# Two SwiGLU down projections as a seven-product 2x2 block product, with two smaller reorderings

## The chip, the core and the metric

The kernel runs on 1 core of one Trainium2 chip. The metric is the device time in microseconds (us) of one launch. TensorE (PE) multiplies, VectorE (DVE), ScalarE (ACT) and GpSimd (POOL) work elementwise, SyncE (SP) issues most of the DMAs. Each engine runs its own queue strictly in order; between engines only semaphores count.

## What is computed

Two transformer-like blocks over 1024 tokens of width 1024, float32. The part that the change rewrites stands at the end of each block:

```python
D_FF = ((8 * D_MODEL + 3 * 256 - 1) // (3 * 256)) * 256          # 2816
def _swiglu(h, w_gate, w_up, w_down):
    return (jax.nn.silu(h @ w_gate) * (h @ w_up)) @ w_down
# block 1
x_new = x_new + g2 * _swiglu(_modulate(x_new, norm_ffn_w[layer], sh2, sc2), w_ffn_gate[layer], w_ffn_up[layer], w_ffn_down[layer])
# block 2: the same form, with h = rms_norm(x) * (1 + sc2) + sh2
x = x + g2 * ((jax.nn.silu(h @ ffn_w_gate[l]) * (h @ ffn_w_up[l])) @ ffn_w_down[l])
```

Two smaller parts are touched too: `hyena_filters` (a small network of sines whose filters are windowed, squared and summed over 1024 positions) and the first norm of block 2, `rms_norm(x) * (1 + sc1) + sh1`.

## The kernel before

Activations lie feature-major: 8 tiles (KT) of 128 features by 1024 tokens, and tokens are cut into two halves of 512 (HALF). The hidden width is 22 tiles (FT). Every float32 product is made of three matmuls of rounded parts: high weights by high activations, high by low, low by high. ACT makes a high part with a rounding copy, DVE makes the low part by subtracting it from the raw tile, so a raw tile always passes ACT and then DVE before PE may use it.

**Gate and up projections** (class `Quad`, used by both ffn stages). For n from 2 to 21 the gate and up product of hidden tile n is already a 2x2 block product with seven products, each of 12 matmuls, in the order p1, p6, p2, p7, p5, p4, p3 on three PSUM banks per n. POOL forms the weight sums of n + 1 (`sums_s124`) and of n + 2 (`sum_s3`) and adds some products to others (lines 2311, 2313, 2315). ACT copies products out of the banks (`copy`, line 2395), because PE adds the next product into the same bank: p4 waits for the copy of p7, p3 for the copy of p5. ACT also applies the silu of token half 0 right after p2 (line 2416); it stands ahead of the copies of p7 and p5. The two hidden halves of n come out on DVE (`direct_out`, `second`), and SP stores each to DRAM (`ffn_hidden`, line 2293). In SP's loop over n the loads of weights for n + 2 stand ahead of the stores of n.

**Down projection** (function `ffn`). It runs in NS = 22 steps: 11 pairs of hidden tiles for token half 0, then 11 for half 1. A step loads 1024 KB of weights (line 2533) and 512 KB of hidden rows (line 2535) into one of three slots; ACT rounds them (`parts_high`, lines 2588 and 2589), DVE makes the low parts (`split`, lines 2611 and 2613), and PE does 48 matmuls of 128x512 (8 output tiles m, 2 hidden tiles, 3 parts) into 8 banks, line 2574 to 2576. The load of step n waits for the end of step n - 3. Steps 0 to 2 are loaded and in part split while `Quad` still runs its last n. After 11 steps DVE adds the 8 banks to x (`evict`, line 2633) and ACT and DVE begin the squares of the next norm. x itself was put aside in DRAM, and one DMA of 4096 KB brings it back right after the load of step 7 (line 2540).

In ffn_1 (block 1) POOL also issues `cond_row` (a row of 512 KB) and 24 DMAs of 1024 KB (`condition_space`, line 2550): the modulation vector of block 2 is computed in the shadow of the down projection, ACT making one silu (line 2593) and DVE two reductions per group (`modulate`, line 2624). ACT's silu stands in its queue between the parts of step 1 and those of step 2. POOL then stores the finished x to `x_kept`, 16 DMAs.

**Start of block 2** (`block_2`, stage "projections"): ACT rounds three loaded weight groups (`proj.highs`) and then the normed x (`norm_2.take_high`); DVE makes the low weight parts (`proj.lows`, line 2971), then scales half 0 of x (line 622), makes its low part (line 626), and does the same with half 1.

**Filter network** (`filter_network`, woven into stage "modulation_1"): for each of 8 position chunks c PE fills banks 4 and 5 (line 826), DVE windows them (line 874), ACT squares them (line 848), PE sums the squares (line 833). The matmul of chunk c waits until DVE has read the banks of chunk c - 1; DVE's write of chunk c waits until the DRAM stores of chunk c - 2 have landed, since the difference is formed in place.

## Time and profile before

| | us |
|---|---|
| median of 3 runs | 3599.43 (3591.16 to 3603.64) |
| the profiled execution | 3592.82, span of its instructions 3590.8 |
| PE busy | 3312.8 (92% of the span), mean granted clock 0.945 |
| DVE, ACT, POOL busy | 1763.1, 1190.3, 553.0 |
| DMA | 366.16 MB, 102 GB/s over the span |

The page gives for every engine its busy time, for every line and tile a group of instructions, and who ended the idle time ahead of it. A matmul's duration there (389 ns) is longer than the distance from one matmul to the next, because matmuls are pipelined, so a stage is costed by the distance.

### The profile page before, as it was taken

How to read it: one execution, taken by the hardware profiler on the slowest of the kernel's cores; microseconds unless marked ns; L12 is line 12 of the kernel's file. 1: busy time of each engine (PE TensorE's matmuls, PEld its weight loads, DVE VectorE, ACT ScalarE, POOL GpSimd, SP SyncE). 2: the span in 40 equal slices, each digit the busy share in tenths (PEclk: the TensorE clock that was granted, in tenths of full speed). 3: DMA queues.
4: the chain of work that ended last, by engine and by line, in shares of the span. 5: the costliest groups of instructions: out<-in, count | busy, mean ns of one | idle time of the engine just before them, and what ended most of it. 6: DMA issues, size and time to landing. Idle time of an engine off the chain costs nothing. (4 is left out here: it accounts for less than half of the span.)

```text
span 3590.8 us, 38285 instructions
## 1 busy us (share of the span) xinstructions
PE 3312.8 (92%) x15192; PEld 2476.6 (69%) x15192; DVE 1763.1 (49%) x2758; ACT 1190.3 (33%) x1829; POOL 553.0 (15%) x560
## 2 busy tenths in 40 slices
PE   7999998988899999999998998888878899999997
PEld 4476544444778778888886777565456678888886
DVE  6447535446323374433576634444665474443344
ACT  3326522212422253333233332441220253333232
POOL 3100000000100024554001010011000025544000
PEclk8999997996899999999999999998989899999999
DMA  5430010000332232223775123233324132222533
GB/s 225 170 129 13 10 36 13 13 13 1 128 120 93 94 109 82 81 87 110 266 271 216 44 70 93 80 108 118 76 94 158 54 103 81 87 81 96 199 141 117
DMA packets 109945, 366.16 MB, mean 102 GB/s; under 512 B 13991, under 2 KB 33447, under 8 KB 91720
## 3 DMA queue, kind: packets, MB, share of 16 engines
q1 hardware_dynamic: 72056, 244.24, 19.3%
q0 software_dynamic: 21056, 111.05, 8.2%
q10 hardware_dynamic: 16656, 8.42, 1.3%
q8 instruction: 121, 1.98, 0.2%
q14 instruction: 56, 0.46, 0.0%
HBM read 300.63 MB, written 63.05 MB: 101 GB/s over the span
## 5 line engine op out<-in xcount | busy, mean ns | idle before, releaser
L2574 PE MATMUL banks<-hidden_high,down_high 128*128 128x512 f32 x704 | 274.9, 390 | 3.8 <-DVE x L2633 3.8
L2576 PE MATMUL banks<-hidden_high,down_low 128*128 128x512 f32 x704 | 273.9, 389 | 0.0
L2575 PE MATMUL banks<-hidden_low,down_high 128*128 128x512 f32 x704 | 273.9, 389 | 0.0
L1585 PE MATMUL banks<-work,weight_ring 128*128 128x512 f32 (+1 forms) x640 | 264.9, 575 | 0.5 <-ACTq L4296 0.5
L2144 POOL TENSOR_TENSOR quad_raw<-quad_raw 128x512 f32<-128x512 f32 x160 | 229.6, 1436 | 126.4 <-DMA quad_raw<-in_w_gu 120.2
L2276 PE MATMUL banks<-block_t_high,quad_low 128*128 128x512 f32 x608 | 236.5, 389 | 0.0
L2611 DVE TENSOR_TENSOR down_low<-down_raw,down_high 128x2048 fp32r<-128x2048 f32 x44 | 100.9, 2292 | 237.0 <-ACT down_high L2588 237.0
L1585 PEld LDWEIGHTS banks<-work,weight_ring 128*128 128x128 f32 x640 | 126.6, 200 | 130.1 <-issue 124.7
L2588 ACT ACTIVATE down_high<-down_raw 128x2048 fp32r<-128x2048 f32 x44 | 84.4, 1918 | 317.2 <-DMA hidden_raw<-ffn_hidden 317.2
L1767 DVE SCALAR_TENSOR_TENSOR x<-x,work,banks 128x128 f32<-128x128 f32 x320 | 111.3, 348 | 142.9 <-PE banks L1611 132.4
L2274 PE MATMUL banks<-block_t_high,quad_high_b 128*128 128x512 f32 x456 | 177.6, 390 | 0.4 <-ACT quad_partial L2395 0.3
L2275 PE MATMUL banks<-block_t_low,quad_high_b 128*128 128x512 f32 x456 | 177.4, 389 | 0.0
L2276 PE MATMUL banks<-block_b_high,quad_low 128*128 128x512 f32 x456 | 177.4, 389 | 0.0
L2395 ACT ACTIVATE quad_partial<-banks 128x512 f32<-128x512 f32 x160 | 95.6, 598 | 241.9 <-PE banks L2276 236.1
L2574 PEld LDWEIGHTS banks<-hidden_high,down_high 128*128 128x128 f32 x704 | 132.2, 188 | 32.3 <-DVE hidden_low L2613 4.6
L2575 PEld LDWEIGHTS banks<-hidden_low,down_high 128*128 128x128 f32 x704 | 132.2, 188 | 27.8 <-issue 0.5
L2576 PEld LDWEIGHTS banks<-hidden_high,down_low 128*128 128x128 f32 x704 | 132.1, 188 | 27.5
L2944 PE MATMUL banks<-mix_high,ring_parts 128*128 128x512 f32 x320 | 134.8, 421 | 13.6 <-DVE ring_parts L2971 4.6
L2474 DVE TENSOR_TENSOR quad_gated<-banks,quad_partial 128x512 f32<-128x512 f32 x40 | 27.7, 692 | 229.6 <-PE banks L2276 224.6
L2194 DVE TENSOR_TENSOR quad_low<-quad_raw,quad_high_a 128x1536 fp32r<-128x1536 f32 x44 | 79.4, 1804 | 106.3 <-POOL quad_raw L2144 104.9
L2276 PEld LDWEIGHTS banks<-block_t_high,quad_low 128*128 128x128 f32 x608 | 114.2, 188 | 23.8
L2945 PE MATMUL banks<-mix_low,ring_parts 128*128 128x512 f32 x320 | 129.2, 404 | 0.0
(607 smaller groups left out, 7497.6 us busy)
## 6 DMA issues: line engine op xcount, KB each, us to landing
down_raw<-in_w_down SPq DMA_DIRECT2D x44, 1024.0 KB, 4.9
quad_raw<-in_w_gu SPq DMA_DIRECT2D x40, 768.0 KB, 4.3
condition_space<-in_mod_w POOLq DMA_DIRECT2D x24, 1024.0 KB, 6.2
ffn_hidden<-quad_gated SPq DMA_DIRECT2D x88, 256.0 KB, 2.0
hidden_raw<-ffn_hidden SPq DMA_DIRECT2D x44, 512.0 KB, 5.9
weight_ring<-in_w_merge SPq DMA_DIRECT2D x24, 512.0 KB, 3.7
quad_raw<-in_w_gu SPq DMA_DIRECT2D x48, 256.0 KB, 3.1
weight_ring<-in_dft SPq DMA_DIRECT2D x12, 1024.0 KB, 5.4
```

The lines of the kernel that those rows point to most:

```text
L1585: mm = e.matmul(pg.ps[:, bank_of(h, n), 0:b - a], slot[:, (2 * k + t) * P:(2 * k + t + 1) * P], h1[:, k, a:b], start=(k == 0), stop=(k == ...
L1767: ins = e.scalar_tensor_tensor(out=S[:, 8 * d + (q + 1) % 8, :], in0=S[:, 8 * d + q % 8, :], scalar=dec[:, d, 4 * t + c:4 * t + c + 1], in ...
L2144: e.tensor_tensor(self.weight(n, out), self.weight(n, a), self.weight(n, b), op).then_inc(self.sums.sem, 1)
L2274: e.matmul(bank, w_hi[:, k], hi[:, k], start=(start and k == 0), stop=False, skip_group_check=again)
L2275: e.matmul(bank, w_hi[:, k], lo[:, k], start=False, stop=False, skip_group_check=again)
L2276: mm = e.matmul(bank, w_lo[:, k], hi[:, k], start=False, stop=(k == 3), skip_group_check=again)
L2574: e.matmul(bank, wh[:, k, m], hh[:, k], start=(p == 0 and k == 0), stop=False)
L2575: e.matmul(bank, wh[:, k, m], hl[:, k], start=False, stop=False)
L2576: mm = e.matmul(bank, wl[:, k, m], hh[:, k], start=False, stop=(p == NP - 1 and k == 1))
L2611: e.tensor_tensor(wl, raw, wh.bitcast(F32), ALU.subtract).then_inc(low.sem, 1)
L2944: e.matmul(bank, w_hi[:, c], MH[:, k, t], start=start, stop=False)
L2945: e.matmul(bank, w_hi[:, c], ML[:, k, t], start=False, stop=False)
```

## The change

**The down projection.** The 1024 outputs are cut into two halves of 512 (4 tiles), each pair of hidden tiles into its two members, the tokens into their two halves. The product of a 2x2 block of weights with a 2x2 block of hidden values is formed with seven block products instead of eight, in four phases of 11 steps (NS = 44): phases 0, 1 and 2 do two products per step (24 matmuls), phase 3 one (12 matmuls). Slots go from three to four; the load of step n waits for the end of step n - 4.

- While `Quad` runs, POOL forms four block combinations of the hidden values for each pair of n (`turn_hidden`), SP stores seven blocks of 256 KB per pair instead of four. The even n's hidden tiles get buffers of their own (`even`), and before these are written again, `out_free` waits for the four combinations and for the stores of the pair.
- POOL forms the weight combinations: two subtractions per step in phase 0, one in phases 2 and 3, none in phase 1 (`weight_sums`). One of phase 0 is stored by SP to DRAM (`down_sum`) and loaded again in phase 3. The load of step n, for n from 4 to 14, waits until the `down_sum` of step n - 4 has been stored; that store is issued right behind the load of step n - 1.
- A step loads 1280 KB in phase 0 (and stores 256 KB), 1024 KB in phases 1 and 2, 768 KB in phase 3.
- After phases 0, 1 and 2 ACT copies the 8 banks out (`stage_products`, 24 copies), POOL adds them to each other (`fold`, 12 additions in its queue at step 23), and DVE adds the results to x (`onto`) at steps 24 to 27, 35, 36 and 38; four banks are added directly at the end.
- x comes back behind the load of step 14. The 24 condition groups are spread one per step over steps 4 to 10, 12 to 21 and 26 to 32; `cond_row` is issued behind the last `turn_hidden`. POOL's `x_kept` stores stand at steps 30 and 41 and at the end.

**The filter network** uses two pairs of banks in turn and a tile of its own for the difference (`filter_bank`, `DIFF`): the matmul of chunk c waits for DVE's read of chunk c - 2, and the wait for the stores stands only ahead of the sum. The modulation's four groups then share two banks, and are read out inside DVE's loop.

**The norm of block 2**: ACT takes the high parts of half 0 ahead of the weights' high parts, and DVE scales half 0 ahead of `proj.lows`, and half 1 behind the low part of half 0.

```diff
@@ Quad
+        self.turned_hidden.wait(e, 4 * (n // 2))            # out_free
+        if s == 0:
+            self.stored[0].wait(e, 16 * (n - 1))
+        else:
+            self.stored[1].wait(e, 80 * (n // 2))
@@ Quad.sync
-            for s in range(2):
-                self.out[s].wait(e, n + 1)
-                e.dma_start(self.hidden[n, :, s * HALF:(s + 1) * HALF], self.pg.gated[:, 2 + s, :]).then_inc(self.stored[s].sem, 16)
+            to = self.hidden[n // 2]
+            self.out[0].wait(e, n + 1)
+            e.dma_start(to[:, BLOCK_21 if n % 2 else BLOCK_11, :], self.out_tile(n, 0)).then_inc(self.stored[0].sem, 16)
+            if n % 2:
+                self.out[1].wait(e, n + 1)
+                e.dma_start(to[:, BLOCK_22, :], self.out_tile(n, 1)).then_inc(self.stored[1].sem, 16)
+                t1, t2, t4 = self.pg.turned
+                for i, (block, tile) in enumerate(((BLOCK_T1, t1), (BLOCK_T2, t2), (BLOCK_T3, self.pg.even[:, 1, :]), (BLOCK_T4, t4))):
+                    self.turned_hidden.wait(e, 4 * (n // 2) + i + 1)
+                    e.dma_start(to[:, block, :], tile).then_inc(self.stored[1].sem, 16)
@@ Quad.pool
+            if n % 2 == 0:
+                self.turn_hidden(e, n - 1)
             self.copied.wait(e, 4 * i + 2)
             e.tensor_tensor(s6, s1, s6, ALU.add).then_inc(self.joined.sem, 1)
...
+            if n == FT - 1:
+                down_sums(e, 1)
+                down_sums(e, 2)
+        self.turn_hidden(e, FT - 1)
@@ Quad.scalar
             self.products.wait(e, self.done(n, "p2"))
-            self.stored[0].wait(e, 16 * n)
-            e.activation(pg.gated[:, 2, :], self.bank(n, 0), ACT.Silu).then_inc(self.silu_1.sem, 1)
+            self.out_free(e, n, 0)
+            e.activation(self.out_tile(n, 0), self.bank(n, 0), ACT.Silu).then_inc(self.silu_1.sem, 1)
             copy(n, 2, "p7")
             copy(n, 3, "p5")
@@ ffn, sync
+                step_done(e, n - SLOTS)
+                if n - SLOTS < NP:
+                    s2_stored.wait(e, 16 * (n - SLOTS + 1))
...
         for n in range(3, NS):
             load(e, n)
-            if n == 7:
+            if n - 3 < NP:
+                sums.wait(e, 2 * (n - 3) + 2)
+                e.dma_start(s2[n - 3], pg.down[(n - 3) % SLOTS][0][:, 2, :]).then_inc(s2_stored.sem, 16)
+            if n == 14:
                 e.dma_start(x, x_kept).then_inc(x_back.sem, 16)
@@ ffn, tensor
+            for i, (wh, w_low, bh, b_low) in enumerate(products):
+                for m in range(4):
...
+                    elif p == 0 and phase:
+                        staged.wait(e, 8 * (phase - 1) + at + 1)
+                    c = slice(m * P, (m + 1) * P)
+                    e.matmul(bank, wh[:, c], bh, start=(p == 0), stop=False)
+                    e.matmul(bank, wh[:, c], b_low, start=False, stop=False)
+                    mm = e.matmul(bank, w_low[:, c], bh, start=False, stop=(p == NP - 1))
@@ block_2, vector
+        norm_2.scale_half(e, 0)
         proj.lows(e, 0)
         norm_2.take_low(e, 0)
+        norm_2.scale_half(e, 1)
         norm_2.take_low(e, 1)
```

Three places where instructions stand in another order now, each of ffn_1 where `Quad` hands over to the down steps. Names such as `projection_full` or `to_fm_sums` in brackets are semaphores that several stages share.

SP's queue there. Before: `ffn_hidden` rows are the hidden stores, `down_raw` and `hidden_raw` the loads.

```order
131 L2533 DMA down_raw_91<-in_w_down 128x2048 [waits projection_full]
132 L2535 DMA hidden_raw_92<-ffn_hidden 128x2x512 [waits chunk_rows_spread_0]
133 L2533 DMA down_raw_97<-in_w_down 128x2048 [waits projection_full]
134 L2535 DMA hidden_raw_98<-ffn_hidden 128x2x512 [waits chunk_rows_spread_0]
135 L2533 DMA down_raw_103<-in_w_down 128x2048 [waits projection_full]
136 L2535 DMA hidden_raw_104<-ffn_hidden 128x2x512 [waits chunk_rows_spread_0]
137 L2293 DMA ffn_hidden<-quad_gated 128x512 [waits chunk_outputs]
138 L2293 DMA ffn_hidden<-quad_gated 128x512 [waits chunk_products]
139 L2533 DMA down_raw_91<-in_w_down 128x2048 [waits projection_group_used]
140 L2535 DMA hidden_raw_92<-ffn_hidden 128x2x512 [waits chunk_rows_spread_0]
141 L2533 DMA down_raw_97<-in_w_down 128x2048 [waits projection_group_used]
```

After: the `ffn_blocks` stores come from the hidden tiles and from the combinations (`hidden_turned`, waiting for `to_fm_sums`), `columns_raw` is the hidden block's load, and `down_sum` the stored weight combination.

```order
169 L2323 DMA ffn_blocks<-quad_gated 128x512 [waits chunk_outputs]
170 L2326 DMA ffn_blocks<-quad_gated 128x512 [waits chunk_products]
171 L2330 DMA ffn_blocks<-hidden_turned_116 128x512 [waits to_fm_sums]
172 L2330 DMA ffn_blocks<-hidden_turned_117 128x512 [waits to_fm_sums]
173 L2330 DMA ffn_blocks<-even_hidden 128x512 [waits to_fm_sums]
174 L2330 DMA ffn_blocks<-hidden_turned_118 128x512 [waits to_fm_sums]
175 L2605 DMA down_raw_106<-in_w_down 128x1024 [waits projection_full]
176 L2606 DMA down_raw_106<-in_w_down 128x512
177 L2620 DMA columns_raw_107<-ffn_blocks 128x1024 [waits chunk_rows_spread_1]
178 L2626 DMA down_sum<-down_raw_91 128x512 [waits to_fm_ready]
179 L2605 DMA down_raw_91<-in_w_down 128x1024 [waits chunk_rows_spread_0,projection_group_used]
180 L2606 DMA down_raw_91<-in_w_down 128x512
```

The load of step 3 (`down_raw_106`) now stands behind six stores of which four wait for POOL, and from there on a store stands behind every load, and the next load waits for it (`chunk_rows_spread_0`).

POOL's queue at the same place. Before: the last additions of `Quad`, then the condition DMAs.

```order
202 L2311 TENSOR_TENSOR quad_partial<-quad_partial 128x512 [waits projection_read]
203 L2313 TENSOR_TENSOR quad_partial<-quad_partial 128x512 [waits projection_read]
204 L2315 TENSOR_TENSOR quad_partial<-quad_partial 128x512 [waits chunk_summed]
205 L2546 DMA condition_space<-in_cond_rows 128x1024 [waits projection_full]
206 L2550 DMA condition_space<-in_mod_w 128x2048 x2
207 L2550 DMA condition_space<-in_mod_w 128x2048 [waits modulation_used] x22
```

After: `down_raw` rows are the weight combinations of steps 1, 2, 3 and 4.

```order
247 L2638 TENSOR_TENSOR down_raw_96<-down_raw_96 128x512 [waits projection_loaded_1]
248 L2640 TENSOR_TENSOR down_raw_96<-down_raw_96 128x512 [waits to_fm_ready]
249 L2638 TENSOR_TENSOR down_raw_101<-down_raw_101 128x512 [waits projection_loaded_2]
250 L2640 TENSOR_TENSOR down_raw_101<-down_raw_101 128x512 [waits to_fm_ready]
251 L2372 TENSOR_TENSOR hidden_turned_116<-even_hidden 128x512 [waits chunk_rows_spread_1,chunk_products,chunk_outputs]
252 L2374 TENSOR_TENSOR hidden_turned_117<-quad_gated,hidden_turned_116 128x512 [waits to_fm_sums]
253 L2375 TENSOR_TENSOR even_hidden<-quad_gated,even_hidden 128x512
254 L2377 TENSOR_TENSOR hidden_turned_118<-quad_gated,hidden_turned_117 128x512 [waits to_fm_sums]
255 L2672 DMA condition_row<-in_cond_rows 128x1024 [waits chunk_products,projection_full]
256 L2667 DMA condition_space<-in_mod_w 128x2048
257 L2638 TENSOR_TENSOR down_raw_106<-down_raw_106 128x512 [waits projection_loaded_3]
258 L2640 TENSOR_TENSOR down_raw_106<-down_raw_106 128x512 [waits to_fm_ready]
```

The condition row is issued behind the combinations of steps 1 and 2 and behind `turn_hidden`.

ACT's queue at the same place. Before:

```order
609 L2588 ACTIVATE down_high_100<-down_raw_97 128x2048 [waits projection_loaded_1]
610 L2589 ACTIVATE hidden_high_102<-hidden_raw_98 128x1024
611 L2399 ACTIVATE quad_gated<-quad_gated 128x512 [waits chunk_states]
612 L2593 ACTIVATE condition_space<-condition_space 128x1024 [waits condition_loaded]
613 L2588 ACTIVATE down_high_106<-down_raw_103 128x2048 [waits projection_loaded_2]
614 L2589 ACTIVATE hidden_high_108<-hidden_raw_104 128x1024
```

After:

```order
609 L2730 ACTIVATE down_high_100<-down_raw_96 128x1024 [waits to_fm_ready,projection_loaded_1]
610 L2731 ACTIVATE down_high_100<-columns_raw_97 128x1024
611 L2457 ACTIVATE quad_gated<-quad_gated 128x512 [waits chunk_states]
612 L2750 ACTIVATE condition_row<-condition_row 128x1024 [waits condition_loaded]
613 L2730 ACTIVATE down_high_105<-down_raw_101 128x1024 [waits to_fm_ready,projection_loaded_2]
614 L2731 ACTIVATE down_high_105<-columns_raw_102 128x1024
```

The order is the same; what moved is what the fourth row waits for: the DMA of the condition row, now behind POOL's `turn_hidden`, stands ahead of the parts of step 2 (`down_high_105`).

## Rows read from the trace of the kernel before

**Rows 1.** Windows of down stages: us, busy (count) by engine, clock, DMA share, GB/s.

```profile
1706.60:1948.40 241.80, 240.32 (x1058) 198.34 (x1057) 150.91 (x189) 69.88 (x59) 20.90 (x39) 1.00 0.70 264
1862.00:1894.00 32.00, 32.00 (x143) 26.51 (x142) 26.73 (x38) 8.60 (x6) 3.19 (x6) 1.00 0.92 351
3383.30:3402.40 19.10, 19.10 (x86) 15.83 (x85) 3.43 (x2) 2.87 (x2) 0.00 (x0) 1.00 0.96 384
1964.10:1968.10 4.00, 3.98 (x10) 3.16 (x11) 4.00 (x7) 4.00 (x7) 0.00 (x0) 0.51 0.03 6
```

**Rows 2.** Groups: busy, mean ns, idle before. Middle row: one line, min/median/max ns.

```profile
L2574 PE MATMUL banks<-hidden_high,down_high 128*128 128x512 f32 x704 | 274.9, 390 | 3.8 <-DVE x L2633 3.8
...
L2144 POOL TENSOR_TENSOR quad_raw<-quad_raw x160: 1279/1293/3415, 1305.7 to 3293.1; 128x512 f32<-128x512 f32 x160
...
L2624 DVE CUSTOM_DVE_ANT_0 condition_space<-condition_space 128x1024 f32<-128x1024 f32 x48 | 58.7, 1223 | 1.5 <-DMA condition_space<-in_mod_w 0.6
```

**Rows 3.** Timelines (start us, us, engine, line), one down step of ffn_2.

```profile
3483.14 0.33 SPq L2533 DMA_DIRECT2D down_raw<-in_w_down  x1
...
3494.02 0.33 SPq L2533 DMA_DIRECT2D down_raw<-in_w_down  x1
...
3489.45 1.92 ACT L2588 ACTIVATE down_high<-down_raw 128x2048 fp32r<-128x2048 f32 x1 [8.15 <-DMA hidden_raw<-ffn_hidden]
3491.28 1.04 ACT L2589 ACTIVATE hidden_high<-hidden_raw 128x1024 fp32r<-128x1024 f32 x1
...
3493.61 1.22 DVE L2613 TENSOR_TENSOR hidden_low<-hidden_raw,hidden_high 128x1024 fp32r<-128x1024 f32 x1
```

**Rows 4.** DMA issues: operation, engine, count, KB each, median us to landing.

```profile
ffn_hidden<-quad_gated SPq DMA_DIRECT2D x88, 256.0 KB, 2.0
...
x<-ffn_x SPq DMA_DIRECT2D x1, 4096.0 KB, 19.2
```

**Rows 5.** Timelines of one n in ffn_1: POOL, DVE, ACT.

```profile
1668.70 4.35 POOL L2144 TENSOR_TENSOR quad_raw<-quad_raw 128x512 f32<-128x512 f32 x3 [1.20 <-DMA quad_raw<-in_w_gu]
...
1673.15 1.76 DVE L2194 TENSOR_TENSOR quad_low<-quad_raw,quad_high_a 128x1536 fp32r<-128x1536 f32 x1 [2.61 <-POOL quad_raw L2144]
1676.23 2.29 DVE L2194 TENSOR_TENSOR quad_low<-quad_raw,quad_high_b 128x2048 fp32r<-128x2048 f32 x1 [1.32 <-ACT quad_high_b L2183]
...
1676.51 0.60 ACT L2416 ACTIVATE quad_gated<-banks 128x512 f32<-128x512 f32 x1 [0.32 <-PE banks L2276]
1679.23 0.60 ACT L2395 ACTIVATE quad_partial<-banks 128x512 f32<-128x512 f32 x1 [2.12 <-PE banks L2276]
```

**Rows 6.** Timelines, POOL and DVE at once, start of ffn_1.

```profile
1305.71 10.13 POOL L2144 TENSOR_TENSOR quad_raw<-quad_raw 128x512 f32<-128x512 f32 x4 [25.08 <-DMA quad_raw<-in_w_gu]
...
1307.89 3.39 DVE L2445 TENSOR_TENSOR block_b<-block_b,block_t 128x2048 f32<-128x2048 f32 x1
```

**Rows 7.** Timelines, start of ffn_1's down stage (DVE, ACT, POOL, SP).

```profile
1710.60 0.69 DVE L2464 TENSOR_TENSOR quad_gated<-quad_gated,quad_partial 128x512 f32<-128x512 f32 x1 [0.70 <-ACT quad_gated L2399]
...
1711.75 1.06 ACT L2593 ACTIVATE condition_space<-condition_space 128x1024 f32<-128x1024 f32 x1 [1.18 <-DMA condition_space<-in_cond_rows]
...
1707.32 0.58 POOL L2546 DMA_DIRECT2D condition_space<-in_cond_rows  x1 [2.02 <-PE banks L2276]
...
1717.93 0.33 SPq L2533 DMA_DIRECT2D down_raw<-in_w_down  x1
```

**Rows 8.** Timelines, start of block 2's projections (DVE, PE).

```profile
1957.71 2.58 DVE L2971 TENSOR_TENSOR ring_parts<-weight_ring,ring_parts 128x1024 fp32r<-128x1024 f32 x2 [4.46 <-ACT ring_parts L2963]
...
1962.47 5.38 DVE L622 SCALAR_TENSOR_TENSOR x<-x,parameters,work 128x512 f32<-128x512 f32 x8
...
1964.12 0.76 PE L2926 MATMUL banks<-mix_high,ring_parts 128*128 128x512 f32 x1 [10.01 <-ACT mix_high L612]
```

**Rows 9.** Timeline of PE in the filter network's loop.

```profile
30.40 3.78 PE L826 MATMUL banks<-work 64*128 64x512 f32 x4 [7.18 <-ACT work L842]
35.63 3.78 PE L826 MATMUL banks<-work 64*128 64x512 f32 x4 [1.45 <-DVE work L874]
```

414 lines of the change are left out of this document (283 added, 131 removed).

## The prediction, made before the changed kernel had run

> **What bounds the kernel now.** I read the windows of the down stages first. In ffn_1's down stage PE is busy 240.3 of 241.8 us, so the stage is bound by its matmuls; DMA is busy 0.70 at 264 GB/s on average [rows 1]. But in a stretch of the same stage in which x and condition groups arrive, DMA is busy 0.92 at 351 GB/s, and where x comes back in ffn_2 it is 0.96 at 384 GB/s: 7.34 MB in 19.1 us, the most that this trace shows. The groups then say what one operation costs: a matmul group of 704 waits 3.8 us in all, for DVE's eviction; a POOL sum of 128x512 takes 1.29 us, 3.4 at the longest; a modulation reduction on DVE 1.22 us [rows 2]. The timeline of one down step gives the pace: loads are issued 10.88 us apart, 48 matmuls, so 0.2267 us each. It also gives the round trip: issued at 3483.14, ACT begins at 3489.45, 6.3 us for 1.57 MB; ACT takes 1.04 and DVE 1.22 us per 1024 columns [rows 3]. A store of 256 KB lands after 2.0 us, x after 19.2 [rows 4]. So the products are worth their full time only if loads, POOL, ACT and DVE keep pace with a shorter stage.
>
> **1. Products.** 22 steps of 48 are 1056 matmuls per stage; 33 steps of 24 and 11 of 12 are 924. 2 x 132 x 0.2267 = **-59.8 us**. PE's down stages would fall from 239.4 to 209.5 each.
>
> **2. The loop over n, even n from 2 to 20.** In one n whose PE step begins at 1668.15, POOL's three sums end at +4.9, DVE's two low parts (1.76 and 2.29) begin there and at +8.1, ACT's silu is at +8.4 and the copy of p7 at +11.1 [rows 5]. New behind POOL's sums are the four operations of `turn_hidden`, 5.2 us, and ACT's silu of an even n waits for all four. POOL and DVE operations with two inputs in SBUF take turns: four POOL sums took 10.13 us while DVE was back to back, where 4 x 1.29 = 5.2 was due, and a DVE operation of 2048 columns took 3.39 against 2.29 [rows 6]. Taking turns, the four and the two low parts end at 4.9 + 5.2 + 4.05 = +14.1; silu and copy of p7 follow, to +15.3. PE wants bank 2 for p4 after five products of 12: 60 x 0.2267 = +13.6. Stall 1.7 per even n, 20 in both ffns: 34. If POOL is not held up its four end at +10.1 and nothing is late: 0. Rows 6 is the nearest row, but there DVE left no gap; I take three quarters, **+25** (0 to +34).
> The Trainium skill (SBUF — State Buffer, Who interferes with whom) says that a DVE instruction with two SBUF inputs and a GpSimd instruction that reads SBUF exclude each other for the whole instruction, and that issue order decides who blocks. Rows 6 agree in the sum and leave the order open. By the rule the term is 34 if DVE comes between, and 0 if POOL's four go first.
>
> **3. Start of the down stage (T0 = 1707.05, one step ahead of the load of step 3).** The last hidden half is out at T0 + 4.3 [rows 7]. After the change the second half of 21 waits for more on DVE and POOL, I take T0 + 6.5; four turned blocks with DVE between, as in 2, end near T0 + 14. The load of step 3 stands behind them on SP: issued at 14.3. Then landing 5.5 (6.3 scaled to less data, upper part latency), POOL's two subtractions 2.6, ACT 2.1, DVE 2.4, of which some overlap: ready at 26.4. PE wants step 3 after 3 x 5.44 = 16.3. ffn_2: **+10** (5 to 12). In ffn_1 the condition row, issued at 1707.32 with its silu at 1711.75 [rows 7], is now issued at T0 + 14; its silu stands on ACT ahead of the parts of step 2, behind which are all later parts. 14 + 4.4 + 1.1 + 2.1 + 2.3 = 23.9 for step 2, due at 10.9: **+13** (8 to 16). Load 3 is ready in its shadow.
>
> **4. Phase 0.** A load waits for the store behind the load before it, so data do not queue: load and store, 1.57 MB, make one round trip of 6.3 us per step [rows 3] where PE wants 24 x 0.2267 = 5.44. 7 steps x 0.86 = **+6** for ffn_2 (0 to 12). In ffn_1 a 1 MB group comes with each step: 2.62 MB at 384 GB/s are 6.8 us, and DVE (2 x 1.22 for the group, 2.4 to split) shares its port with POOL's 2.6. I take 8 us per step: 7 x 2.5 = **+17** (10 to 25).
>
> **5. x comes back** behind load 14. 4.2 MB at 384 GB/s are 10.9 us. The loads behind have no lead left after 4; in ffn_2 a step of phase 1 needs 2.7 us of transfer and has 5.44, so half of it is regained: **+5** (0 to 11). In ffn_1 load and group are 2.1 MB, 5.46 us, so nothing is regained, and the rest of the row competes: **+14** (5 to 16).
> The Trainium skill (DMA: Bandwidth & Descriptors, Specifications) gives about 358 GB/s for one core's share of HBM. Rows 1 show 384, so the measurement decides; by the page's figure each 2.1 MB would take 5.9 us, and this term with the one before about 8 us more.
>
> **6. Sums on POOL.** At its step 23 stand 12 additions, 15.6 us, ahead of the weight sum of step 24. The copies start them about 1 us into step 22; sum, ACT and DVE follow (4.6): ready at +21, due at +10.9. What of the copies' lead and of DVE's reads can be regained I put at 3: **+7** each, +14 (6 to 20). Phase 2 of ffn_1 has, at steps 26 to 28, split 2.4, reductions 2.45, additions of x 2 x 0.6 and more on DVE, and 1.3 on POOL, over 5.44: **+8** (0 to 12). Phase 3 has steps of 2.72 us in which DVE has 1.8 and POOL 1.3, and four additions or squares, and eight spills of POOL, stand between: **+9** for both (3 to 15).
> The stage boundaries: three times one ACT copy (0.60) per ffn, 3.6, for the 3.8 us that the eviction cost [rows 2]: 0.
>
> **7. Norm and filter.** DVE's three low parts of weights stand ahead of the scaling of half 0, which begins at 1962.47 and can begin near 1953, when ACT's and DVE's first group is done; PE waits 10.0 us there [rows 8]. The high parts of the weights now come later, so that of the wait only about 4 go: **-3.9** (-8 to 0). PE restarts at a clock of 0.51 of the full 2.4 GHz (the 1.2 GHz level) for 4 us after that idle time [rows 1]. In the filter loop PE's 3.78 us are followed by 1.45 of waiting for DVE [rows 9]; with two pairs of banks it goes, but ACT and DVE then set the pace: **-1.5** (-6 to 0).
>
> **Sum:** -59.8 + 25 + 10 + 13 + 6 + 17 + 5 + 14 + 14 + 8 + 9 - 3.9 - 1.5 = +55.8. The profiled execution is 3592.8 (span 3590.8 and 2 around it), 6.6 under the median of 3599.4, inside the runs' spread. 3592.8 + 55.8 = 3648.6; against the median, which I forecast, **3655**.
>
> **Rivals.**
> *B. Half of the waits.* POOL's four go first (2 becomes 0), and the four slots cover a part of 4 and 5: waits 75 of 121, with -65 that is +10: 3605 to 3615. For it: a POOL sum is 1.29 us in the median, with 3.4 as rare end [rows 2], so POOL is seldom held up. Against: its sums are ahead of DVE's parts there, `turn_hidden` stands beside them.
> *C. Faster: the saving stands.* Its place is the load of step 3 and the chain of loads and stores behind it. It decides if load 3 is issued by T0 + 8, and a load and its store together land within 5.44 us: a store of 256 KB alone lands after 2.0 [rows 4], and it waits in SP's queue only for a POOL sum done long ago. Then 4 is 0, 3 is 8 in all, 5 is 8, 2 is 0, and 6 half, 16: 32 against -65.2, **3566**. If ffn_1 is then bound by its bytes (47.9 MB of blocks, 25 of groups, 8 of x, 81 at 384 GB/s: 211 us for 209.5) that adds 2. Against it: the 6.3 us of rows 3 hold for 1.57 MB whoever asks.
> *D. The transfers bind ffn_1 over its whole length.* 81 MB at the 351 GB/s of the mixed stretch are 231 us, 21 over PE's 209.5, on top of a late start: with 2 and 6 in full, 3690 or more.
> *E. The change does not do what it says:* 132 matmuls fewer per ffn are countable, so only in that a clock fall after the new waits takes from the rest: over 10 us of waiting costs 4 us at 0.51 again, in 3, twice: +4.
>
> **How the numbers follow.** My case, most waits in full, 3620 to 3700: 0.55. B 0.15, of which half lies within 0.3% (10.8 us, about what a measurement of this kernel can tell from no change). C 0.22, D 0.06, E's addition 0.02. Faster by over 0.3%: C and a little of B, **0.24**; within: **0.08**; slower: **0.68**. Both signs have weight, so: the likeliest case alone is 3620 to 3700; the range leaves the lower half of C and the end of D out: **3563 to 3694**.
>
> **What will show it.** PE's count in the down lines must fall by 264. Term 2: idle of PE ahead of p4 on ACT's copy of p7 in even n, and `turn_hidden` operations well over 1.3 us. Term 3: a gap on PE at T0 + 16.3 in ffn_2 of about 10, and in ffn_1 at T0 + 10.9 of 13, ended by DVE's low parts. Term 4: loads issued 6.3 and 8 us apart in phase 0, each right after a store has landed; if they are 5.44 apart the term is 0. Term 5: a gap near steps 15 to 18, DMA at 0.95. Term 6: a gap at step 24 behind POOL. Term 7: PE's wait at block 2 down from 10 to 6. The prediction is wrong if PE's idle time inside the down stages is under 40 us, or in the loop over n under 5.

## The result: 3730 us, 3.8% slower

The changed kernel takes 3730.4 us (median of 4 runs, 3723.7 to 3734.7) against 3595.3 for the kernel before: 1.0375 times its time, 95% interval 1.0341 to 1.0409. Slower was the likelier forecast, but the time lies above the range; the change costs 135 us where the sum said 56. The experiments below find where the 135 us went; no kernel with the seven-product down projection, however mended, came under the kernel before.

The page of after, first its engine line and two groups of part 5 (busy, mean ns | idle ahead, releaser), then a DMA row (KB, us to landing):

```profile
PE 3307.7 (89%) x14928; PEld 2453.4 (66%) x14928; DVE 1871.4 (50%) x2900; ACT 1238.3 (33%) x1965; POOL 884.0 (24%) x760
...
L2710 PE MATMUL banks<-down_high 128*128 128x512 f32 x616 | 259.9, 422 | 123.9 <-DVE columns_low L2781 87.8
...
L2304 PE MATMUL banks<-block_t_high,quad_high_b 128*128 128x512 f32 x456 | 179.8, 394 | 17.2 <-ACT quad_partial L2453 17.2
...
condition_space<-in_mod_w POOLq DMA_DIRECT2D x24, 1024.0 KB, 8.2
```

PE has 264 matmuls fewer, as meant, and is hardly less busy (3307.7 us for 3312.8). Ahead of the down matmuls it idles 123.9 us, where the group of before had 3.8 [rows 2], and one matmul takes 422 ns in the mean for 390, since a part of them ran at the low clock (the stages' mean granted clock is 0.89 and 0.93, where before it was 1.00). The windows of the two down stages (columns as in [rows 1]):

```profile
1723.20:2036.00 312.80, 238.40 (x927) 187.35 (x925) 198.82 (x259) 99.53 (x128) 98.99 (x96) 0.89 0.72 255
3436.00:3712.80 276.80, 227.24 (x927) 180.92 (x926) 133.70 (x139) 99.95 (x129) 80.41 (x57) 0.93 0.55 184
```

ffn_2's before, which [rows 1] do not show:

```profile
3327.90:3570.50 242.60, 240.24 (x1059) 198.28 (x1058) 89.39 (x69) 68.70 (x57) 0.00 (x0) 1.00 0.39 143
```

ffn_1's down stage took 241.8 us before [rows 1] and takes 312.8, and ffn_2's went from 242.6 to 276.8. From the starts of the stages in the two traces, the 142.1 us between the spans (3590.8 and 3732.9) are: everything up to the first gate and up product, the filter network in it, -2.4; gate and up projections +18.7 and +18.8; ffn_1's down stage with the norm behind it +68.8; the untouched rest of block 2 +4.1; ffn_2's down stage with the tail +34.1.

**Excess.** A step of the down stage has an ideal length (24 matmuls of 0.2267 us, 5.44 us; in phase 3 it is 12, 2.72 us). What the distance between two steps' first matmuls is over that is called its excess here, low clock included. It is worked out from the start of every step in the trace, and summed over steps:

```
steps          0-3   4-10  11-13 14-22 23-25 26-32 33-43  all
after   ffn_1 17.1   34.6   2.0  17.5  13.0   6.2  12.9  103.4
        ffn_2 15.2   20.1   1.9   5.1  13.3   0.0  11.5   67.2
```

That is 170.6 us of excess for 59.8 us of matmuls saved (an execution of `silu_behind`, whose down stages are the same code, has 168.8). A delay is counted in the step ahead of the matmul that it holds: an excess in step 10 is a late start of step 11. In between, steps run at exactly 5.44: the product saving is real, and it is lost at named places.

### The profile page after: what moved, and what is told of

Read it like the earlier page. It is cut to its first block and busy times, and to the rows that moved or that the text cites. A ratio compares the mean times of both kernels' runs of the same rounds, so it can differ in the third digit from the quotient of the medians.

```text
span 3732.9 us, 38599 instructions
## 1 busy us (share of the span) xinstructions
PE 3307.7 (89%) x14928; PEld 2453.4 (66%) x14928; DVE 1871.4 (50%) x2900; ACT 1238.3 (33%) x1965; POOL 884.0 (24%) x760
## 5 line engine op out<-in xcount | busy, mean ns | idle before, releaser
L2710 PE MATMUL banks<-down_high 128*128 128x512 f32 x616 | 259.9, 422 | 123.9 <-DVE columns_low L2781 87.8
L2711 PE MATMUL banks<-columns_low,down_high 128*128 128x512 f32 x616 | 252.6, 410 | 0.0
L2712 PE MATMUL banks<-down_high,down_low 128*128 128x512 f32 x616 | 252.2, 409 | 0.0
L2710 PEld LDWEIGHTS banks<-down_high 128*128 128x128 f32 x616 | 123.8, 201 | 166.2 <-DVE columns_low L2781 97.2
L2304 PE MATMUL banks<-block_t_high,quad_high_b 128*128 128x512 f32 x456 | 179.8, 394 | 17.2 <-ACT quad_partial L2453 17.2
L1781 DVE SCALAR_TENSOR_TENSOR x<-x,work,banks 128x128 f32<-128x128 f32 x320 | 111.3, 348 | 139.2 <-PE banks L1625 128.7
L2730 ACT ACTIVATE down_high<-down_raw 128x1024 fp32r<-128x1024 f32 x66 | 69.8, 1057 | 322.6 <-POOL down_raw L2640 135.1
L2224 DVE TENSOR_TENSOR quad_low<-quad_raw,quad_high_a 128x1536 fp32r<-128x1536 f32 x44 | 97.4, 2213 | 106.2 <-POOL quad_raw L2174 104.9
L1868 POOL DMA_DIRECT2D branches<-work x32 | 17.3, 541 | 557.1 <-ACT work L1939 554.7
L3145 PE MATMUL banks<-mix_high,ring_parts 128*128 128x512 f32 x320 | 137.1, 428 | 13.5 <-DVE ring_parts L3172 4.5
L2712 PEld LDWEIGHTS banks<-down_high,down_low 128*128 128x128 f32 x616 | 123.3, 200 | 28.0
L2711 PEld LDWEIGHTS banks<-columns_low,down_high 128*128 128x128 f32 x616 | 124.4, 202 | 26.2 <-issue 0.5
```

Source lines behind the costliest of these rows:

```text
L1781: ins = e.scalar_tensor_tensor(out=S[:, 8 * d + (q + 1) % 8, :], in0=S[:, 8 * d + q % 8, :], scalar=dec[:, d, 4 * t + c:4 * t + c + 1], in ...
L2224: e.tensor_tensor(flat(pg.w_low[n % 2][:, a:b]), pg.w_raw[n % 2].big[:, a * HALF:b * HALF], flat(high).bitcast(F32), ALU.subtract).then_in ...
L2304: e.matmul(bank, w_hi[:, k], hi[:, k], start=(start and k == 0), stop=False, skip_group_check=again)
L2710: e.matmul(bank, wh[:, c], bh, start=(p == 0), stop=False)
L2711: e.matmul(bank, wh[:, c], b_low, start=False, stop=False)
L2712: mm = e.matmul(bank, w_low[:, c], bh, start=False, stop=(p == NP - 1))
```

## The experiments

Each kernel is compared with the kernel before in runs on the same chip. The time is the median, then comes its ratio to the kernel before with the 95% interval. The intervals reach 4 to 18 us to each side, so smaller differences between two kernels are not told by the times. Excess rows have the columns of the table above.

**Low clock: a cost, or a companion of the waits?** The granted clock is 0.5 in many short stretches of the new down stages. `fill` repeats eight matmuls per step in steps 0 to 9, into banks whose result is then not the reference's:

```diff
+                    if n < 10 and i == len(products) - 1 and m == 3:
+                        before = slice((m - 1) * P, m * P)
+                        for _ in range(8):
+                            e.matmul(pg.ps[:, at - 1, :], wh[:, before], bh, start=False, stop=False, skip_group_check=True)
```

> The changed kernel with eight extra matmuls (repeats of the group before, into its bank) ahead of the last group of each of steps 0 to 9 of both down stages; the output is no longer the reference's in those banks. 160 matmuls more, 36 us at 0.2267 each. The trace of the changed kernel has in steps 0 to 10 an excess over 24 x 0.2267 of 52 us in ffn_1 and 35 us in ffn_2, and 33 and 17 us of stretches at 0.5 clock in them. Theory A (PE's short waits lower its clock, and the low clock is a cost of its own beside the wait): the added work lies in the waits, keeps PE busy, low-clock stretches in these steps fall to under half, and the kernel gets faster by 5 to 15 us although it computes more. Theory B (the loads set the pace, the low clock only lies beside the waits): time unchanged within 5 us. Theory C (PE's work is on the path there): 36 us slower.

3736.6 us against 3595.5, ratio 1.0402 (1.0364 to 1.0440): 6.2 us over the changed kernel by the medians, inside both intervals. Windows of steps 0 to 10 of ffn_1 and ffn_2, first of the changed kernel (columns as above):

```profile
1723.20:1834.80 111.60, 74.70 (x265) 57.39 (x264) 49.18 (x71) 26.24 (x28) 35.27 (x33) 0.83 0.70 240
3436.00:3531.20 95.20, 68.16 (x265) 52.87 (x265) 33.76 (x36) 25.21 (x27) 31.38 (x23) 0.90 0.57 178
```

And of `fill`:

```profile
1717.30:1828.60 111.30, 84.10 (x346) 66.02 (x344) 50.27 (x71) 26.31 (x28) 36.05 (x33) 0.95 0.71 242
3427.50:3522.90 95.40, 82.23 (x346) 64.86 (x344) 33.81 (x36) 25.28 (x27) 31.36 (x23) 0.98 0.57 178
```

80 more matmuls per stage, the clock up from 0.83 to 0.95 and from 0.90 to 0.98, and the same 111 and 95 us. Theory A falls (nothing got faster), C falls (36 us), and B holds as far as the noise lets it be told: in this stretch neither the low clock nor 18 us of added work per stage sets the pace. What does is shown by the next kernel. (Low clock does cost where the loads are ahead: step 24 of ffn_2 in after runs 1.6 us over its 5.44 behind an idle gap of 11.5.)

**Phase 0's chain of stores and loads.** `store_first`:

```diff
         for n in range(3, NS):
-            load(e, n)
             if n - 3 < NP:
                 sums.wait(e, 2 * (n - 3) + 2)
                 e.dma_start(s2[n - 3], ...).then_inc(s2_stored[(n - 3) % 2].sem, 16)
+            load(e, n)
```

> The changed kernel with SP issuing the down_sum store of step n - 3 ahead of the load of step n, not behind it (two semaphores in turn, since two stores are then under way at once). Theory A (phase 0's pace of 7.5 to 8.5 us per step is the round trip of load, store and wait, since the wait for the store behind a load empties the transfer queue): loads then follow at 5.44 us in ffn_2, the excess of its steps 4 to 10 (20.1 us) falls under 5, that of ffn_1's (34.6 us) to 5 to 20, where the condition groups compete; in all 25 to 45 us faster. Theory B (POOL's two sums with DVE's splits, or the bytes, set that pace): both stay within 5 us of what they were.

3669.7 us, 1.0208 (1.0174 to 1.0242): 61 us faster than the changed kernel, the largest single gain and more than the 25 to 45 expected. By the traces 53 of it are excess of the two down stages:

```
store_first 1 18.3    7.6   0.0  12.2  13.5   7.3  16.0   75.0
            2 16.6    0.0   0.1   0.4  13.9   0.0  11.5   42.4
```

SP's timeline in phase 0 of ffn_2, of after:

```profile
3491.32 0.33 SPq L2605 DMA_DIRECT2D down_raw<-in_w_down  x1
...
3492.65 0.43 SPq L2626 DMA_DIRECT2D down_sum<-down_raw  x1
3498.83 0.33 SPq L2605 DMA_DIRECT2D down_raw<-in_w_down  x1
```

And of `store_first`:

```profile
3445.07 0.33 SPq L2605 DMA_DIRECT2D down_raw<-in_w_down  x1
...
3450.51 0.33 SPq L2605 DMA_DIRECT2D down_raw<-in_w_down  x1
...
3455.95 0.33 SPq L2605 DMA_DIRECT2D down_raw<-in_w_down  x1
```

In after, the store is issued 1.33 us behind the load's first part and the next load goes 6.18 us after the store: 7.51 per step. With the store ahead it is 5.44, PE's pace. A holds. A store then takes no less time (7.1 us in the median of these three steps), but the load behind it no longer waits for it. The loads then have lead when x comes back, and its gap in ffn_2 (5.1) goes too.

Not all of phase 0's excess is the pace of the loads. In ffn_2 the split of step 11 has ended on DVE at 3524.98 and PE is done with step 10 at 3525.5, and yet step 11 starts at 3531.22:

```profile
3523.76 1.22 DVE L2781 TENSOR_TENSOR columns_low<-columns_raw,down_high 128x1024 fp32r<-128x1024 f32 x1
...
3528.59 1.06 ACT L2730 ACTIVATE down_high<-down_raw 128x1024 fp32r<-128x1024 f32 x1 [5.05 <-DMA columns_raw<-ffn_blocks]
...
3530.50 3.98 ACT L2741 ACTIVATE down_staged<-banks 128x512 f32<-128x512 f32 x8
...
3531.22 0.76 PE L2710 MATMUL banks<-down_high 128*128 128x512 f32 x1 [5.68 <-ACT down_staged L2741]
```

The first product of phase 1 needs a bank that ACT has to copy out, and these copies stand in ACT's queue behind the parts of step 12, which wait for the load of step 12. PE waits 5.7 us for them in each ffn (the excess of step 10 is 7.4 and 6.0). With the store first the load of step 12 is early and the wait is gone. Putting the copies ahead of the parts of step 12 was not tried.

**The start of the down stage.** `load3` puts the load and the sums of step 3 ahead of the last turned blocks, `cond_late` moves ACT's silu of the condition row behind the parts of step 4.

```diff
+            if n == FT - 1:
+                down_load(e, 3)
             if n % 2:
                 self.out[1].wait(e, n + 1)
...
                 down_sums(e, 2)
+                down_sums(e, 3)
         self.turn_hidden(e, FT - 1)
```

> The changed kernel with the load of step 3 ahead of the last pair's store of its second half and of the four turned blocks on SP, and POOL's weight sums of step 3 ahead of the last turn_hidden. Theory A (the first gaps of the down stage come from turn_hidden and its stores standing ahead of load 3): ffn_2's excess of steps 2 and 3 (10.5 us) falls to 2 to 5; ffn_1's steps 1 and 2 (11.8 us) stay or grow by 2.6, since there the condition row's silu is what holds ACT. Theory B (what holds steps 1 to 3 is ACT, DVE and POOL taking turns on the splits): nothing falls by more than 2 us in either.

```diff
-        if mod:
-            row_loaded.wait(e, 16)
-            e.activation(pg.cond_row, pg.cond_row, ACT.Silu).then_inc(row_ready.sem, 1)
         for n in range(2, NS):
             parts_high(e, n)
+            if mod and n == 4:
+                row_loaded.wait(e, 16)
+                e.activation(pg.cond_row, pg.cond_row, ACT.Silu).then_inc(row_ready.sem, 1)
```

> The changed kernel with ACT's silu of the condition row behind the parts of step 4, not ahead of those of step 2 (DVE's wait for it moves to its first reduction). Theory A (in ffn_1 the row's transfer, issued behind turn_hidden, holds the parts of step 2): ffn_1's excess of steps 1 and 2 (11.8 us with its low clock) falls by 4 to 9, after which load 3 is late as in ffn_2 (10.5 us in steps 2 and 3), so that only 1 to 5 us of the kernel are gained. Theory B (the row is not what is waited for): nothing changes in any step.

3727.6 us, 1.0367 (1.0317 to 1.0417), and 3728.2 us, 1.0367 (1.0337 to 1.0397): neither gains anything that these runs can tell. `load3` takes 3 us off steps 0 to 3 of ffn_2 (15.2 to 12.2), and its gap of 7.5 us stands at the end of step 3, no longer at step 2's: SP now issues load 3 early and load 4 behind the same stores. `cond_late` takes ffn_1's steps 0 and 1 from 13.7 to 4.7 us and puts steps 2 and 3 from 3.4 to 14.4. Both theories A are right about the cause of a gap, not about its size afterwards (2 to 5 us expected in ffn_2's steps 2 and 3, 7.5 measured): both edits move it to the next thing in the same queue. ACT in after, at the row's silu:

```profile
1743.17 1.06 ACT L2750 ACTIVATE condition_row<-condition_row 128x1024 f32<-128x1024 f32 x1 [12.99 <-DMA condition_row<-in_cond_rows]
1744.14 1.04 ACT L2730 ACTIVATE down_high<-down_raw 128x1024 fp32r<-128x1024 f32 x1
```

ACT waits 13 us for the row with the parts of step 2 behind it.

**The loop over n.** `silu_behind`: for even n, ACT's silu stands behind the copies of p7 and p5.

```diff
+            if n % 2:
+                silu_1()
             copy(n, 2, "p7")
             copy(n, 3, "p5")
+            if n % 2 == 0:
+                silu_1()
```

> The changed kernel with ACT's silu of token half 0, for even n alone, behind the copies of p7 and p5, not ahead. Theory A (the loop over n lost 18.7 us per ffn because that silu waits for the four turned blocks, and PE's p4 waits for the copy of p7 behind it): 15 us per ffn come back, 25 to 35 us in all. Theory B (POOL and DVE taking turns delays the low weight parts, and PE waits for those next): under 10 us in all.

3692.9 us, 1.0270 (1.0246 to 1.0294): 37.5 us faster. That is as much as the loops had lost, but in part by chance: by the traces the two loops take 32.9 us less (432.3 and 430.1 us for 447.7 and 447.6; 428.9 and 428.7 before), and the rest lies in stages of the same code. PE's waits for ACT's copies (us in total, times, longest), in `silu_behind`:

```profile
PE banks L2296 <- ACT quad_partial L2453: 5.0, 4, 1.8
PE banks L2304 <- ACT quad_partial L2453: 2.0, 1, 2.0
```

7.0 us for 31.9 in after (14.7 at L2296, 17.2 at L2304). A holds, and B, under which the low weight parts would have been the next to be late, falls. About 5 us of the loops' loss stay.

**The fold.** `fold_spread` puts POOL's additions in fours behind the sums of steps 24, 25 and 26; `thin_fold` leaves them where they are and makes them 8 columns wide.

```diff
-            if n == 2 * NP + 1:
-                fold(e)
+            if 2 * NP + 2 <= n < 2 * NP + 5:
+                fold(e, n - 2 * NP - 2)
```

> The changed kernel with POOL's 12 fold additions in three fours, behind the weight sums of steps 24, 25 and 26, not all ahead of the sums of step 24. Theory A (the gap at steps 23 and 24, 13.0 us in ffn_1 and 13.3 in ffn_2 with its low clock, is POOL's queue): both gaps fall under 3 us, 20 to 26 us faster in all; DVE's onto may be late by 2 to 3 us at steps 24 to 27. Theory B (the gap is the load of step 24 or DVE): within 5 us of before.

3725.0 us, 1.0360 (1.0312 to 1.0408). ffn_2's gap is 9.9 us for 13.3, ffn_1's 12.9 for 13.0, and it comes one step later, which neither theory had. The sums of step 25 now stand behind four additions, and DVE's first additions to x, which wait for the fifth and sixth, stand ahead of the split of step 25.

```diff
-                e.tensor_tensor(a[:, i, :], a[:, i, :], b[:, i, :], ALU.add).then_inc(folded.sem, 1)
+                e.tensor_tensor(a[:, i, 0:8], a[:, i, 0:8], b[:, i, 0:8], ALU.add).then_inc(folded.sem, 1)
```

> The changed kernel with POOL's 12 fold additions on 8 of 512 columns each, all else in place, so the sums that DVE adds to x are not complete. Spreading the additions took the gap in steps 23 to 25 only from 13.3 to 9.9 us in ffn_2 and moved it one step on. Theory A (POOL's 15.6 us of additions, and DVE waiting for them ahead of its next split, are the gap): it falls under 2 us in both ffns, 23 to 26 us in all. Theory B (the 16 additions to x on DVE, 11 us, are enough to make it): 4 us or more stay in each.

This kernel leaves out most of the sums that are added to x. 3700.5 us, 1.0296 (1.0267 to 1.0325): 30 us faster than the changed kernel, 24 of it in the two down stages; steps 23 to 25 are at 0.0 in both ffns, and ffn_1's steps 26 to 32 rise from 6.2 to 10.2. So POOL's additions are the gap, and the additions to x alone do not make one in these steps. The timelines of POOL and DVE around it, in after:

```profile
3608.64 4.92 POOL L2656 TENSOR_TENSOR down_staged<-down_staged 128x512 f32<-128x512 f32 x4
3613.52 4.93 POOL L2642 TENSOR_TENSOR down_raw<-down_raw 128x512 f32<-128x512 f32 x4
```

```profile
3615.95 3.59 DVE L2776 TENSOR_TENSOR down_low<-down_raw,down_high 128x1024 fp32r<-128x1024 f32 x1 [17.17 <-ACT down_high L2730]
```

After the fold, POOL makes four steps' sums in a row, and DVE's split of step 24, which is due, waits beside them: 3.59 us for 1.22 [rows 3], 2.4 of the gap of 11.5.

**Phase 3.** `thin_sum3`: POOL's subtraction on 8 columns, so that most of phase 3's weights are left as they were loaded.

```diff
-                e.tensor_tensor(w[:, 1, :], w[:, 0, :], w[:, 1, :], ALU.subtract).then_inc(sums.sem, 1)
+                e.tensor_tensor(w[:, 1, 0:8], w[:, 0, 0:8], w[:, 1, 0:8], ALU.subtract).then_inc(sums.sem, 1)
```

> The changed kernel with POOL's subtraction of phase 3 on 8 of 512 columns, all else in place, so phase 3's weights are not the right ones. Phase 3 has an excess of 12.9 us in ffn_1 and 11.5 in ffn_2 over steps of 2.72 us. Theory A (POOL's 1.3 and DVE's 1.37 us take turns, 2.67 of 2.72, so everything else on DVE comes on top): the excess falls to 2 to 6 us each, and DVE's operations of 1.7 us fall back to 0.68. Theory B (DVE's own work, the additions to x and the squares, or ACT's: these are enough): it falls by under 3 us each.

3716.8 us, 1.0341 (1.0311 to 1.0372). Steps 33 to 43 fall from 11.5 to 4.9 us in ffn_2, from 12.9 to 8.5 in ffn_1. DVE's group of one split of phase 3 (busy, mean ns), in after and, second, in `thin_sum3`:

```profile
L2779 DVE TENSOR_TENSOR columns_low<-columns_raw,down_high 128x512 fp32r<-128x512 f32 x22 | 19.4, 880 | 0.0
```

```profile
L2779 DVE TENSOR_TENSOR columns_low<-columns_raw,down_high 128x512 fp32r<-128x512 f32 x22 | 15.0, 684 | 0.0
```

A holds for ffn_2: 6.6 of its 11.5 us come from POOL's subtraction, 4.9 stay without it. In ffn_1 8.5 stay; what ffn_1 has more in phase 3 was not found. No condition group is loaded or reduced there; POOL's stores of x at step 41, which only ffn_1 has, were not tested.

**The two small parts alone.** `norm_filter` is the kernel before with them and the old down projection, the core of it being

```diff
-                if c:
-                    e.wait_ge(f_cp, c)
+                if c >= 2:
+                    e.wait_ge(f_cp, c - 1)
...
+        norm_2.scale_half(e, 0)
         proj.lows(e, 0)
         norm_2.take_low(e, 0)
+        norm_2.scale_half(e, 1)
```

> The kernel before with only the two small changes (filter network, norm order of block 2), the old down projection. By the traces of before and after: the stretch up to the first gate and up product is 2.4 us shorter, the one from the last down matmul to the first projection of block 2 is 2.1 us shorter, but block 2 from there to its ffn is 4.1 us longer in the changed kernel. Theory A (these 4.1 us are the down change's doing or chance): 3 to 5 us faster than before. Theory B (they come with the norm order): within 2 us of before.

3585.6 us, ratio 0.9970 (0.9958 to 0.9981), 12 runs against 17: 10 us faster than the kernel before, a small gain but clear of the noise, where A expected 3 to 5. The wait of PE at the start of block 2:

```profile
1957.91 0.80 PE L2933 MATMUL banks<-mix_high,ring_parts 128*128 128x512 f32 x1 [7.50 <-DVE ring_parts L2978]
```

That matmul starts 6.2 us earlier than in [rows 8]: 3.8 had been gained before the wait, 2.4 come from it (7.50 for 10.01), and 1.5 more in the projections behind it, 3.9 in all. The filter's part is 0.9 (PE's last matmul group of it starts at 97.02 us for 97.94). These are 4.8 us of the traces and 10 (7 to 15) of the medians; where the rest of the 10 lies is open, since the other differences between the two traces are in stages that are the same code. That block 2 is 4.1 us longer in after does not come with the norm order: from the last down matmul of ffn_1 to the first gate and up product of ffn_2 it is 941.2 us here, 952.4 in after and 941.1 in `silu_behind`, which all have that order, and 950.4 before. Single traces of the same code differ there by up to 11 us. B falls.

**All moves.** `all_moves` joins the five moves above.

> All five moves at once (store ahead of load, silu of the row late, load and sums of step 3 early, fold spread, silu of even n behind the copies). If the waits named are what the change lost and none takes another's place: 170.6 us of excess in the down stages fall to about 70 (x coming back 18, staging 4, steps 26 to 32 6, phase 3 25, start 10, rest of ffn_1's phase 0 10), and 30 of 37 us in the loop over n return: about 130 us faster than the changed kernel, 3600, the kernel before. If transfers bind ffn_1 (81 MB), its down stage stays over 231 us and the kernel over 3620.

3637.6 us, 1.0114 (1.0093 to 1.0134): 93 us of the 135 are back, not the 130 expected. `store_first` (61) and `silu_behind` (37.5) alone sum to 98, so the other three moves add nothing to them: the excess is 112.3 us, not 70, since the gap at the start, now at step 3, and that of the fold only moved.

```
all_moves   1 17.9   10.7   0.0  10.9  12.0   8.6  14.0   74.0
            2 14.0    2.0   0.0   0.6   9.9   0.3  11.5   38.3
```

`v2` also stores the last pair's blocks behind load 5, with POOL's last `turn_hidden` behind the sums of step 4, and folds two per step; `v3` brings x back in eight parts.

```diff
+            if n == 6:
+                quad.store_turned(e, FT - 1)
...
-            if n == 2 * NP + 1:
-                fold(e)
+            if 24 <= n < 30:
+                fold(e, n - 24)
...
-            if 24 <= n < 28:
+            if n in (26, 28, 30, 32):
```

> All moves once more, with two changed: the last pair's second half and turned blocks are stored behind load 5 and POOL's last turn_hidden stands behind the sums of step 4 (loading step 3 early alone only moved the gap to step 3's end, where load 4 stood behind those stores); the fold is two additions per step in steps 24 to 29, and DVE adds to x at steps 26, 28, 30 and 32. Theory A (queue order makes these gaps): steps 2 to 5 fall from 17 to 5 in ffn_1 and from 10 to 3 in ffn_2, steps 23 to 32 from 21 and 10 to 8 and 3: 30 us under all_moves, 3608. Theory B (POOL and DVE taking turns bounds the stretch from 23 on, whatever the order): steps 23 to 32 keep 15 and 8 us, 3620.

```diff
-            if n == 14:
-                e.dma_start(x, x_kept).then_inc(x_back.sem, 16)
+            if 14 <= n < 22:
+                e.dma_start(x[:, n - 14, :], x_kept[:, n - 14, :]).then_inc(x_back.sem, 16)
```

> The kernel v2 with x coming back as eight DMAs of 512 KB, one behind each of the loads of steps 14 to 21, not as one of 4096 KB behind load 14. Theory A (ffn_1's gap at steps 14 and 15, 8.9 us in all_moves, is the one long transfer ahead of load 15): it falls under 2 us and little appears later, 5 to 8 us faster than v2. Theory B (with a condition group per step ffn_1 is at its byte limit there, 2.6 MB in 5.44 us are 480 GB/s): the gap is spread over steps 14 to 22 and its sum stays within 3 us.

3631.7 us, 1.0094 (1.0069 to 1.0120), and 3628.2 us, 1.0094 (1.0071 to 1.0116). The times of `all_moves`, `v2` and `v3` can't be told apart; what follows is read from one trace each.

```
v2          1  4.2   18.4   0.0  16.6   0.0  21.1  17.9   78.2
            2  5.9    6.2   0.0   0.7   0.0   3.8  11.5   28.1
v3          1  4.1   18.3   0.0  13.1   0.0  21.4  15.3   72.2
            2  4.5   10.0   0.0   0.2   0.0   3.9  11.6   30.2
```

ffn_2's down stage is now 237.6 us and shorter than the 242.6 of before. ffn_1's is 287.7. There the fold's gap of 12.0 came back as 12.5 more in steps 26 to 32, and the gap at the start as one of 9.3 at step 5, where the stores now stand. For the stretch from step 23 on theory B is right for ffn_1 (21.1 us, 15 expected) and theory A for ffn_2 (3.8); at the start A's 5 us for ffn_1's steps 2 to 5 became 13.5. The kernel's 3608 were missed by 24. In `v2`, steps 23 to 32 of ffn_1:

```profile
1890.00:1958.00 68.00, 54.30 (x208) 42.38 (x207) 67.31 (x77) 21.62 (x30) 34.08 (x25) 0.90 0.64 227
```

DVE is busy 67.3 of 68.0 us, a part of that waiting beside POOL's 34.1. That no order of the queues would help here is argued from this row, not tried. Of `v3`, B is the nearer: with x in parts, steps 14 and 15 fall from 10.7 to 0.4 us and steps 16 to 22 rise from 6.0 to 12.6, in sum 3.5 less.

**What ffn_1 has more of.** Both on `v2`: `thin_red` does the reductions on 8 of 1024 columns, `thin_cond` loads 64 of 1024 columns of each condition group from the third on. In both the modulation vector of block 2 is not the right one.

```diff
-                e.tensor_tensor_reduce(pg.cond_products, pg.cond_slots[g % 2][:, t, :], pg.cond_row, ...
+                e.tensor_tensor_reduce(pg.cond_products[:, 0:8], pg.cond_slots[g % 2][:, t, 0:8], pg.cond_row[:, 0:8], ...
```

> The kernel v2 with DVE's 48 condition reductions on 8 of 1024 columns, the groups still loaded in full; the modulation vector of block 2 is not complete then. In v2 ffn_2's down stage has 28.1 us of excess and ffn_1's 78.2, in the latter 18.4 in steps 4 to 10, 16.7 in 14 to 22, 21.1 in 26 to 32, 17.9 in phase 3. Theory A (ffn_1 is slower by DVE's 1.22 us reductions, which take turns with POOL): the four fall together by 25 to 40 us, most in steps 26 to 32. Theory B (the groups' 25 MB beside the blocks' are the cause): under 10 us.

```diff
-            e.dma_start(pg.cond_slots[g % 2], ...)
+            k = T if g < 2 else 64
+            e.dma_start(pg.cond_slots[g % 2][:, :, 0:k], ...)
```

> The kernel v2 with the condition groups from the third on loaded in 64 of 1024 columns only (some 22 MB less in ffn_1), the reductions in full; the modulation vector of block 2 is wrong then. Theory A (DVE's reductions): ffn_1's excess of 78.2 us falls by under 10. Theory B (transfers): steps 14 to 22 (16.7 us) fall to about 1 as in ffn_2, steps 4 to 10 from 18.4 to about 6, and 25 us or more go in all.

3613.4 us, 1.0044 (1.0000 to 1.0088), and 3627.2 us, 1.0089 (1.0068 to 1.0110).

```
thin_red    1  4.3   20.5   2.6   8.8   0.0   9.8  14.4   60.4
thin_cond   1  3.2   18.8   0.0   4.2   0.0  21.7  13.5   61.4
```

By the traces the reductions are 17.8 us, most in steps 26 to 32 (21.1 to 9.8), and the transfers 16.8, most in steps 14 to 22 (16.6 to 4.2). Of these, 3.5 and 4.4 lie in phase 3, where there is neither a reduction nor a group (ffn_1's phase 3 is 12.9 to 17.5 us in nine traces of the same phase 3 code, so this is within chance): about 14 and 12 us are left of the 50 that ffn_1 has over ffn_2. The medians bear out the first (18 us under `v2`) and not the second (4.5 us, and 2 by the ratios, each of which is known to 8 or 9 us). `v2` was profiled in its slowest execution and `thin_cond` in its fastest.

Steps 4 to 10 fall in neither. But `thin_cond` leaves the row and the first two groups in full, and these are what runs beside the load of step 6. In `v2` that load is issued at 1742.08, the row and the two groups from 1741.11 to 1744.86, and POOL can use the load at 1754.89. The window (columns as in [rows 1]) and POOL's row:

```profile
1742.10:1754.90 12.80, 10.02 (x38) 7.75 (x37) 5.06 (x8) 2.95 (x3) 3.27 (x5) 0.87 0.99 375
1754.89 1.27 POOL L2650 TENSOR_TENSOR down_raw<-down_raw 128x512 f32<-128x512 f32 x1 [9.45 <-DMA columns_raw<-ffn_blocks]
```

The DMAs are busy 0.99 of that time at 375 GB/s. So the excess of 9.3 us in step 5 stands beside full DMAs, and neither kernel tests it; 4.2 of it stand in ffn_2 too, which has no groups.

## Why the prediction was wrong

The step that failed most is term 4, the cost of phase 0: the forecast took 6.3 us per step for load and store together, and the wait of the load for the store in the middle costs 7.5; and it put the boundary between two phases at nothing, where PE waits 5.7 us in each ffn. The mechanisms were otherwise mostly the right ones, and the sizes failed. Forecast and trace (us, both ffns; the loop and steps from the trace of after):

```
term                       forecast  measured
1 products                   -59.8     -59.8
2 loop over n                +25       +37.5
3 start, steps 0 to 3        +23       +32.3
4 phase 0, steps 4 to 10     +23       +54.7
5 x back, steps 14 and 15    +19       +17.9
  ffn_1, steps 16 to 22        0        +4.7
6 fold, steps 23 to 25       +14       +26.3
  ffn_1, steps 26 to 32       +8        +6.2
  phase 3                     +9       +24.4
  staging, steps 11 to 13      0        +3.9
7 norm; filter              -3.9;-1.5  -3.9;-0.9 (alone)
```

The measured rows sum to 143 us. About 6 of these the kernel before had too (241.8 and 242.6 us for 239.4 each), and in the trace of after the small parts brought next to nothing, which leaves the 142.1 between the spans.

- **Term 4 failed most,** 32 us short. The round trip was taken from the first issue of a load to ACT's start, 6.3 us for 1.57 MB. But the store is the fourth DMA of a step: it is issued 1.33 us later and lands last, 6.2 us after its own issue. The cycle is 7.5 us, which the forecast's own statement of the chain (a load waits for the store behind the load before it) gives only if the 1.33 us of issues are added to the store's own time behind the loads, 6.2 us and not the 2.0 of [rows 4]. Seven such cycles are 14.5 us of ffn_2's 20.1. The other 5.7 are PE's wait for ACT's copies at the start of step 11, for which the forecast has 0 ("the stage boundaries": it compared the time of a copy with that of the old eviction, and not what stands ahead of the copy in ACT's queue). The bounds of 0 to 12 for ffn_2 did not hold the 20.1. In ffn_1 8 us per step were taken and 10.4 came in the mean, 34.6 against 17, with 5.7 of the same wait in it; how the rest divides between groups, reductions and the store is not shown in this kernel. With the store first 7.6 are left.
- **Term 6, fold and phase 3,** 28 us short. The 3 us taken off for lead were not there, DVE waits 2.4 beside POOL's own four steps of sums, which follow in one piece, and the low clock behind the gap takes 1.6 and 3.0 more. In phase 3 the forecast wrote down 1.8 us of DVE and 1.3 of POOL for a step of 2.72 and did not add them up. Without POOL's part 6.6 and 4.4 us of the 24.4 go; the rest is the other work there, DVE's additions to x among it, and was not taken apart.
- **Term 2,** 12.5 short. Its wait per even n was over-sized (1.7; it was 0.96 in 18 cases), but the first even n, while the loop is being filled, was taken as one of 20: silu there waits 6.6 us for POOL in each ffn, and 14.7 us of PE's waits are at L2296, with those at L2304 31.9 of the 37.5; the other 5.6 were not traced. POOL's four operations took 8.6 us for 5.2, so the turns themselves were right:

```profile
1331.88 1.29 POOL L2372 TENSOR_TENSOR hidden_turned<-even_hidden 128x512 f32<-128x512 f32 x1
1333.25 2.69 POOL L2374 TENSOR_TENSOR hidden_turned<-quad_gated,hidden_turned 128x512 f32<-128x512 f32 x1
1335.89 3.31 POOL L2375 TENSOR_TENSOR even_hidden<-quad_gated,even_hidden 128x512 f32<-128x512 f32 x1
1339.17 1.26 POOL L2377 TENSOR_TENSOR hidden_turned<-quad_gated,hidden_turned 128x512 f32<-128x512 f32 x1
```

- **Term 3,** 9 short. The load of step 3 and the condition row are the causes that were named, but 4.7 and 4.5 us at step 0 (PE waits there 2.8 us for the last hidden outputs on DVE) had no term. The row took 7.1 us from issue to silu, for 4.4 in [rows 7].
- **Terms 5 and 7** came out near their numbers. That x back costs anything in ffn_2 hangs on term 4, as the forecast said: with the store first it costs 0.4. Term 5's total is luck in part: ffn_1's steps 16 to 22, where nothing was forecast, have 4.7 more. And 3.9 and 0.9 us are read from one trace each, while the medians give 10 for both.
- **The rivals.** C (faster) asked that load and store land within 5.44 us. They do not (6.9 and 7.1 us in the median of three steps even of `store_first`); what is needed is that the next load does not wait for them, and even then the sum stays above the kernel before. B (half of the waits) falls with term 2: POOL was held up. E's +4 for the clock was low: the steps behind the gaps at 14 and 23 lose 1.6, 1.7, 1.6 and 3.0 us, 7.9 in all, beside whatever part of step 0's excess is clock. But by `fill` the low clock of phase 0, which shows most in the trace, is no cost of its own. D (3690 or more) is the nearest in its number, by another cause: ffn_1's DMAs are busy 0.72 of the stage at 255 GB/s, not bound over its whole length, and thinning its groups takes 12 to 17 us off one trace of `v2` and less off the medians.
- **The range** ended at 3694, below the forecast's own terms: with all of them at their upper bounds the sum is about 3713. The measured time is over that too, because phase 0, fold, phase 3, start and loop each passed their own bound. These share one trait: each was costed with the other users of POOL, DVE, ACT's queue and SP away. That this is the reason is a reading of the terms, not a measurement.

## What to carry over

A saving on the engine that bounds a kernel shortens every step, and so takes slack from every other engine: before counting it, add up per step what POOL and DVE need together, what SP must issue and wait for, and what must land, and compare each sum with the new, shorter step. A cycle of DMAs is costed from issue to issue, and where a wait for a store stands ahead of a load, issuing the store first is worth trying before anything else. A gap that is taken away at one instruction often stands at the next one in the same queue: here `load3`, `cond_late` and `fold_spread` each found the right cause and gained nothing that could be told from noise.

## What was not expected of the hardware

- 80 matmuls added to a stage with many short waits cost no time (111.3 for 111.6 us, 95.4 for 95.2) and raised its mean granted clock from 0.83 to 0.95 and from 0.90 to 0.98.
- POOL and DVE do not always alternate. Beside `turn_hidden` one DVE operation stood between two of POOL's, but DVE's operation of 1.22 us that started at 3615.95 lasted until 3619.54, 1.1 us after POOL's row of four sums had ended at 3618.45: two of POOL's sums went ahead of it. The Trainium skill (SBUF — State Buffer, Who interferes with whom) says that such a pair contends for an exclusive lock and that issue order decides who blocks. The lengths here agree with the lock; which of the two comes next is not settled by these traces.
